# Attention layer of a decoder step on one core: decode queries padded by POOL into the input's place, two turns of cache chunks moved between the last prompt units, one cache copy issued two pairs of heads earlier

## The reference, cut to what matters

```python
DIL_WINDOWS = (128, 512, 2048)
DIL_RATES = (1, 4, 16)

def odd_mixer(x, w_in, w_out, past):
    proj = jnp.einsum('btd,de->bte', x, w_in).reshape(B, T, N_DIL, 3, DIL_HEADS, HEAD_DIM)
    for g in range(N_DIL):
        q, k, v = proj[:, :, g, 0], proj[:, :, g, 1], proj[:, :, g, 2]
        if past is None:
            o, lse = dilated_prompt_attention(q, k, v, win, dil, slopes)
        else:
            k_all = jnp.concatenate([kv_buf[:, :, 0].astype(k.dtype), k], axis=1)
            v_all = jnp.concatenate([kv_buf[:, :, 1].astype(v.dtype), v], axis=1)
            o, lse = strided_window_decode(q[:, :, :, None], k_all, v_all, n_past, win, dil, slopes)
            new.append(jnp.stack([k_all[:, T:], v_all[:, T:]], axis=2))
```

## Time and profile before

| What | us |
|---|---|
| median of three executions | 1773.56 (1771.61 to 1775.28) |
| profiled execution, device time | 1772.61 |
| its span, first to last instruction | 1770.80 |
| prompt part of layer 1 ends (`turn(7)`) | 1003.6 |
| first group's values read by DVE L1951 | 1086.55 |
| second group's values read by DVE L1951 | 1129.36 |

### The profile page before, as it was taken

One profiled execution on the slowest core, in us unless ns is written; L12 is line 12 of the kernel. 1 busy time (PEld: TensorE's weight loads), 2 busy tenths in 40 slices (PEclk: granted clock), 3 DMA queues, 4 the chain that ended last, 5 costly groups with the idle time before them and its releaser, 6 DMA issues.

```text
span 1770.8 us, 29064 instructions
## 1 busy us (share of the span) xinstructions
PE 1639.3 (93%) x11306; PEld 887.4 (50%) x11306; DVE 493.0 (28%) x1318; ACT 440.0 (25%) x847; POOL 260.7 (15%) x663
## 2 busy tenths in 40 slices
PE   7889699999999999989999757879999999999996
PEld 5655444544444454536577544444545454444542
DVE  4342512222221222231022422442222222212224
ACT  1422412222222222231022312242222222222223
POOL 0100321112121211100110200042111121212110
PEclk9958899999999999998999888989999999999998
DMA  9962479999999999949982898428998899999990
GB/s 277 283 231 73 173 287 377 360 354 376 353 371 357 371 359 367 362 153 356 336 340 80 289 327 304 200 112 358 362 372 359 354 376 354 370 359 369 360 368 28
DMA packets 114177, 540.78 MB, mean 305 GB/s; under 512 B 19093, under 2 KB 22933, under 8 KB 79956
## 3 DMA queue, kind: packets, MB, share of 16 engines
q1 hardware_dynamic: 110864, 481.67, 70.7%
q0 software_dynamic: 3200, 58.41, 9.6%
q10 hardware_dynamic: 68, 0.08, 0.0%
HBM read 535.69 MB, written 59.58 MB: 336 GB/s over the span
## 4 chain that ended last, share of the span: by engine, by line
PE 86%; DVE 6%; DMA 4%; ACT 1%; issue 1%; SPq 1%; DVEq 0%; PEldq 0%; ACTq 0%
PE ps L1279 25%; PE ps L1299 13%; PE ps L1254 12%; PE ps L1309 10%; PE ps L1563 6%; PE ps L454 3%; PE ps L1569 2%; PE ps L978 2%; PE ps L1316 2%; DMA arena<-in_router_bias 2%; DMA arena<-in_cache_dil_kv 1%; PE ps L1806 1%; PE ps L1685 1%; PE ps L1888 1%; PE ps L1264 1%
## 5 line engine op out<-in xcount | busy, mean ns | idle before, releaser
L1279 PE MATMUL ps<-ring,arena 128*64 128x512 f32 x2048 | 450.4, 592 | 1.6 <-ACT arena L1366 1.6
L1279 PEld LDWEIGHTS ps<-ring,arena 128*64 128x64 f32 x2048 | 147.8, 137 | 292.2 <-issue 290.4
L1299 PE MATMUL ps<-ring,arena 128*64 128x512 f32 x1024 | 233.8, 598 | 0.9 <-ACT arena L1371 0.9
L1254 PE MATMUL ps<-arena 128*128 128x128 bf16 (+1 forms) x3584 | 223.3, 219 | 2.1 <-issue 2.1
L1254 PEld LDWEIGHTS ps<-arena 128*128 128x128 bf16 (+1 forms) x3584 | 207.2, 98 | 18.7 <-issue 18.0
L1309 PE MATMUL ps<-arena 128*128 128x512 bf16 x768 | 179.8, 384 | 5.6 <-DVE arena L1437 5.6
L1366 ACT ACTIVATE arena<-ps 128x512 f32<-128x512 f32 x128 | 76.4, 597 | 359.4 <-PE ps L1254 359.4
L1242 POOL TENSOR_SCALAR arena<-arena 128x64 bf16<-128x64 f32 x384 | 160.2, 444 | 14.0 <-POOLq L1239 14.0
L1234 POOL COPY arena<-misc 128x64 f32 x64 | 15.3, 238 | 847.3 <-POOLq L1231 847.3
L1309 PEld LDWEIGHTS ps<-arena 128*128 128x128 bf16 x768 | 70.4, 98 | 134.7 <-issue 53.1
L1413 DVE CAST arena<-ps 128x256 bf16<-128x256 f32 x64 | 27.2, 425 | 390.7 <-PE ps L1264 390.7
(11 more groups left out here) (323 smaller groups left out, 1366.8 us busy)
## 6 DMA issues: line engine op xcount, KB each, us to landing
ring<-in_w_exp_gate SPq DMA_DIRECT2D x128, 1024.0 KB, 8.0
ring<-in_w_exp_up SPq DMA_DIRECT2D x128, 1024.0 KB, 10.2
ring<-in_w_exp_down SPq DMA_DIRECT2D x128, 1024.0 KB, 7.1
out_dil_kv_sample<-in_cache_dil_kv POOLq DMA_DIRECT2D x8, 4080.0 KB, 35.3
ring<-in_w_in_odd SPq DMA_DIRECT2D x6, 3072.0 KB, 22.6
out_dil_kv_sample<-in_cache_dil_kv POOLq DMA_DIRECT2D x8, 2032.0 KB, 30.2
ring<-in_cache_dil_kv SPq DMA_DIRECT2D x4, 2048.0 KB, 11.5
ring<-in_cache_dil_kv SPq DMA_DIRECT2D x32, 256.0 KB, 8.7
```

The costliest lines, as they stand in the source:

```text
L1254: ins = pe.matmul(ps[:, TOK_A + hf, (c % 4) * P:(c % 4 + 1) * P], lhs, pm[0:m, q, k // 3, :], start=k == 0, stop=k == 6)
L1279: ins = pe.matmul(ps[64 * u:64 * u + CAP, WORK, :], MO["xg"][:, c, u * CAP:(u + 1) * CAP], w[:, c], start=c == 0, stop=c == NC - 1)
L1299: ins = pe.matmul(ps[64 * u:64 * u + CAP, TOK_A + hf, :], MO["hT"][:, j, 64 * u:64 * u + CAP], w[:, j, hf * BANK:(hf + 1) * BANK], start=j ...
```

## The change

- `qz1` now lies in `xT`, and POOL makes it: `od_dec_prepare(pool)` runs in POOL's program ahead of the stores of pair 3. It waits for the last query tile, clears `xT`, copies the 24 blocks; then it waits for the stores of pair 2 (`s_kst[0]` at 16*12) and copies `kns`, which takes their place.
- The four chunks of the first cache now all lie in `W`, over `kst`, `p_s` and `p_pt`. SP issues them after the last `turn(7)` and the stores of pair 3.
- PE turns chunk 0 between pauses 14 and 15, and chunk 1 in two halves around the last values. Turned tiles go through PSUM banks 2 and 3, scores of the decode part to banks 0 and 1. ACT and DVE copy them between their own pauses; the first such copy waits for `s_qz1` at 26 and for the last unit's scores.
- POOL issues the copy of the middle cache ahead of the stores of pair 2, with no wait of its own.

```diff
-        qz1 = W[:, 0:3072].rearrange("p (g i r) -> p g i r", g=3, i=4)
+        qz1 = xflat.rearrange("p (g i r) -> p g i r", g=3, i=4)
...
-        g1c = [xflat[:, 0:D], xflat[:, D:2 * D], xflat[:, 2 * D:3 * D], W[:, 3584:3584 + D]]
+        g1c = [W[:, 384 + b * D:384 + (b + 1) * D] for b in range(4)]
...
             pause(14)
+            od_dec_turn(pe, 0, 0)
             pause(15)
+            od_dec_turn(pe, 0, 1, (0, 1))
             values(15)
+            od_dec_turn(pe, 0, 1, (2, 3))
             turn(7)
...
+            pool.wait_ge(s_op, LAST_QK + 1)
+            pool.memset(xflat, 0.0).then_inc(s_qz1, 1)
...
+            pool.wait_ge(s_kst[0], 16 * 12)
+            pool.tensor_copy(kns, OD["k"][:, :, :, NPR:NT]).then_inc(s_qz1, 1)
...
+            if g == 0 and ck == 0:
+                eng.wait_ge(s_qz1, 26)
+                eng.wait_ge(s_s, 32)
...
-            sp.wait_ge(s_op, LAST_QK + 1)
+            sp.wait_ge(s_ot, 2 + 8)
+            sp.wait_ge(s_kst[1], 16 * 12)
             for b in range(4):
-                if b == 3:
-                    sp.wait_ge(s_qz1, 26)
                 sp.dma_start(chunk_of(b, 4), rows_of(b, 4)).then_inc(s_g1[b], 16)
...
+                if i == 2:
+                    shift(o[names[2][0]], a[names[2][1]], names[2][2])
+                if i == 3:
+                    od_dec_prepare(pool)
                 for part in range(3):
                     item_copied(pool, at_item["k", i, part])
...
-            pool.wait_ge(s_ring[1][slot_of(9)], loaded(1, 9))
-            shift(o[names[2][0]], a[names[2][1]], names[2][2])
...
-                    od_dec_prepare(v)
                     od_dec_dve(v)
```

More of the change, by code:

```diff
@@ L1488, in build @@
         mx1, nb1, den1, rin1 = (gbf[:, 11 * P + 16 * k:11 * P + 16 * k + 16] for k in range(4))
-        qz1 = W[:, 0:3072].rearrange("p (g i r) -> p g i r", g=3, i=4)
-        kns = W[:, 3072:3456].rearrange("p (g i n) -> p g i n", g=3, i=4)
-        sm1 = W[:, 3456:3472]
+        xflat = xT[:, :, :].rearrange("p c t -> p (c t)")
+        qz1 = xflat.rearrange("p (g i r) -> p g i r", g=3, i=4)
+        kns = W[:, 0:384].rearrange("p (g i n) -> p g i n", g=3, i=4)
+        sm1 = W[:, 4480:4496]
         QK = OD["qk"].rearrange("p a g n -> p (a g n)")
@@ L1498, in build @@
         o_all, o_own, o_twice = W[:, 4608:5120], W[:, 5120:5184], W[:, 5184:5312]
-        xflat = xT[:, :, :].rearrange("p c t -> p (c t)")
-        g1c = [xflat[:, 0:D], xflat[:, D:2 * D], xflat[:, 2 * D:3 * D], W[:, 3584:3584 + D]]
+        g1c = [W[:, 384 + b * D:384 + (b + 1) * D] for b in range(4)]
         s1 = mixT[:, 4:8, :].rearrange("p j t -> p (j t)")[:, 0:DEC_W]
@@ L1599, in od_stage_pe @@
             pause(14)
+            od_dec_turn(pe, 0, 0)
             pause(15)
+            od_dec_turn(pe, 0, 1, (0, 1))
             values(15)
+            od_dec_turn(pe, 0, 1, (2, 3))
             turn(7)
-            items_copied(pe, len(OD_ITEMS) - 1)
+            pe.wait_ge(s_qz1, 26)
             pe.wait_ge(s_otc, 2 + 8)
@@ L1635, in od_items_copy @@
             pause(14)
+            od_dec_keys(eng, copy, parity, 0, 0)
             pause(15)
+            od_dec_keys(eng, copy, parity, 0, 1)
         def od_stage_dve(v):
@@ L1767, in odd_prompt_act, with od_dec_prepare @@
             return exps, copy, turned
[L1769 to L1775, removed]
+        def od_dec_prepare(pool):
+            pool.wait_ge(s_op, LAST_QK + 1)
+            pool.memset(xflat, 0.0).then_inc(s_qz1, 1)
+            pool.wait_ge(s_qz1, 1)
+            for n in (LAST_QK, LAST_QK - 1, LAST_QK - 2):
+                item_copied(pool, n)
             q8 = qz1.rearrange("p g i (b h t) -> p g i h b t", h=NH, t=TS)
@@ L1781, in od_dec_prepare, with od_dec_turn @@
                         rows = slice(HD * s, HD * s + HD)
-                        v.tensor_copy(q8[rows, g, i, 2 * i + s], src[rows]).then_inc(s_qz1, 1)
-            v.tensor_copy(kns, OD["k"][:, :, :, NPR:NT]).then_inc(s_qz1, 1)
-            v.wait_ge(s_qz1, 26)
+                        pool.tensor_copy(q8[rows, g, i, 2 * i + s], src[rows]).then_inc(s_qz1, 1)
+            pool.wait_ge(s_qz1, 25)
+            pool.wait_ge(s_kst[0], 16 * 12)
+            pool.tensor_copy(kns, OD["k"][:, :, :, NPR:NT]).then_inc(s_qz1, 1)
         def kt_copied(n):
             return s_kt_copied[n % 2], n // 2 + 1
[L1789 to L1795, removed]
+        def od_dec_turn(pe, g, ck, bbs=range(4)):
+                for bb in bbs:
                     n = 28 * g + 4 * ck + bb
+                    if n < 2:
+                        items_copied(pe, len(OD_ITEMS) - 1)
                     if g == 0 and ck == 0:
@@ L1805, in turn, with od_dec_pe @@
                     for i in range(4):
-                        ins = pe.transpose(ps[:, n % 2, i * P:(i + 1) * P],
+                        ins = pe.transpose(ps[:, 2 + n % 2, i * P:(i + 1) * P],
                                            chunk_of(4 * g + bb, ck)[:, i * P:(i + 1) * P], ident)
                     ins.then_inc(s_kt, 1)
-            turn(0, 0)
+        def od_dec_pe(pe):
+            turn = lambda g, ck: od_dec_turn(pe, g, ck)
             for g in range(2):
@@ L1816, in scores @@
                         pe.wait_ge(s_sm1, 1)
-                    bank, col, gg = (2, ck * P, 1) if ck < 4 else (3, (ck - 4) * P, 0 if ck == 4 else 2)
+                    bank, col, gg = (0, ck * P, 1) if ck < 4 else (1, (ck - 4) * P, 0 if ck == 4 else 2)
                     for i in range(4):
@@ L1826, in od_dec_pe @@
                 for ck in range(7):
-                    if ck < 6:
+                    if ck < 6 and (g or ck):
                         turn(g, ck + 1)
@@ L1833, in od_dec_pe @@
                     for i in range(4):
-                        ins = pe.matmul(ps[:, 3, 384 + 32 * gg:416 + 32 * gg], qz1[:, gg, i, P * g:P * g + P],
+                        ins = pe.matmul(ps[:, 1, 384 + 32 * gg:416 + 32 * gg], qz1[:, gg, i, P * g:P * g + P],
                                         kns[:, gg, i, :], start=i == 0, stop=i == 3)
@@ L1842, in od_dec_pe @@
                     pe.wait_ge(s_otc, 2 + 8)
-                    od_out_pe(pe, 0, range(3))
+                    od_out_pe(pe, 1, range(3))
                 pe.wait_ge(s_ex1, g + 1)
@@ L1871, in od_dec_pe @@
                     pe.sem_inc(s_free[1][slot_of(6 + 4 * g + bb)], 1)
-            od_out_pe(pe, 1, range(3))
+            od_out_pe(pe, 0, range(3))
             outputs_t(pe, 1)
@@ L1911, in od_dec_keys @@
                     eng.wait_ge(s_sd1, 8 * g + max(ck - 1, 0))
-                copy(kt1[:, ck % 2, bb], ps[:, n % 2, :].rearrange("p (i n) -> p i n", i=4)).then_inc(
+                copy(kt1[:, ck % 2, bb], ps[:, 2 + n % 2, :].rearrange("p (i n) -> p i n", i=4)).then_inc(
                     s_kt_copied[parity], 1)
@@ L1924, in od_dec_dve @@
             for g in range(2):
-                for ck in range(g, 7):
+                for ck in range(1 if g else 2, 7):
                     od_dec_keys(v, v.tensor_copy, 1, g, ck)
@@ L1941, in od_dec_dve @@
                 step(v.scalar_tensor_tensor(out=s1, in0=dd1, scalar=row_slope,
-                                            in1=banks(2, DEC_W), op0=ALU.mult, op1=ALU.add))
+                                            in1=banks(0, DEC_W), op0=ALU.mult, op1=ALU.add))
                 step(v.tensor_reduce(c(0), s1, AX.X, ALU.max))
@@ L2136, in _ @@
                 load(1, 6 + b, parts + [(chunk_of(b, ck), rows_of(b, ck)) for ck in (5, 6)])
-            sp.wait_ge(s_op, LAST_QK + 1)
+            sp.wait_ge(s_ot, 2 + 8)
+            sp.wait_ge(s_kst[1], 16 * 12)
             for b in range(4):
-                if b == 3:
-                    sp.wait_ge(s_qz1, 26)
                 sp.dma_start(chunk_of(b, 4), rows_of(b, 4)).then_inc(s_g1[b], 16)
+            sp.wait_ge(s_qz1, 26)
             sp.dma_start(dd1, a["c_odd"][0]).then_inc(s_dd1, 16)
```

## The result

| | before | changed |
|---|---|---|
| median, us | 1772.59 (4 executions) | 1755.40 (4 executions) |
| ratio of the two, 95% interval | 1 | 0.9904 (0.9888 to 0.9920) |
| profiled execution, device time | 1772.61 | 1752.50 |
| its span | 1770.8 | 1750.7 |

The change makes the kernel 17.2 us faster; the interval of the ratio allows 14.2 to 19.9 us. The forecast was 25.6 us (1747) in a range from 1737 to 1758, so the sign and the range hold and the size is too large by 8 us. Part of the span's 20.1 us comes from ahead of the change: pair 1's last store was issued at 945.12 and is now issued at 943.22, 1.9 us earlier, in a stretch where both programs are the same. Instants of the two profiles differ by that much.

The account below looks back on a forecast made before the run. It took SP's transfers, starved by the middle cache's copy, as the bound. Transfer 9 at 1013, tail 9.7 and first group 38.45 put the values' reader at 1061.2 instead of 1086.55: 25.3 off 1772.6, forecast 1747, range 1737 to 1758.

Parts of the forecast that it names:

- The bound and the mechanism: Layer 1: the copy starves SP's queue; issued at 945.7 it lands near 1002, and PE waits for transfer 9 until 1013.
- One sign of being wrong: PE standing where `s_qz1` decides, over 4 us waiting for chunks or second keys, or slower prompt tiles between 946 and 981.
- The packet count that gave 1013: Transfers 8 and 9: of 1536 packets, 1000 remain at 1002 and need 9.2 us; about 2 us added for engines finishing unevenly.
- POOL's part: `qz1` memset 2.9 us and 24 copies 5.7 us, then `kns`; `s_qz1` at 26 at about 1006, hidden behind 1013.
- Rival 4: Slower than before because POOL's small copies are the bound; 1790 at 3 us each; 3%.
- The prompt's tail: Last weights to last turn: 4.3 us, plus tiles 3.0, DVE copy 0.7, waits 0.5, clock 1.2; 9.7 together, ending at 1022.7.
- The first group: First scores to the values' reader: 22.35, 7.0 and 9.1, sum 38.45 us, so read at 1061.2 instead of 1086.55.
- under cover: After the prompt: SP's chunk 4 covered by 1 us, second group's keys by a hair; range keeps up to 6 us for both.
- The sum: Whole kernel: 25.3 us off 1772.6 gives 1747.3; the shown median is 0.95 above the profiled execution; stated as 1747.
- Rival 1: Queues share by bytes, so stores behind the copy and `kns` decide, `s_qz1` at 1008 to 1013; 1744 to 1748; 10%.

Follow-up runs that it names:

- run 3: The changed kernel with the middle cache's copy one place earlier still, behind the first cache's copies after pair 0: 1733.61 us, ratio 0.9793.
- run 8: The changed kernel once more without any further edit, beside a repeat of the copy's move alone: 1748.13 us, ratio 0.9893.
- run 1: The kernel before with only the middle cache's copy moved ahead of pair 2's stores: 1752.27 us, ratio 0.9902.
- run 2: The changed kernel with the copy back at its old place behind the last stores: 1771.67 us, ratio 1.0007.
- run 7: The changed kernel with chunks 0 and 1 turned after the prompt again: 1745.44 us, ratio 0.9861.
- run 4: The changed kernel with the same copy in pieces of 4064 bytes, 16 DMAs of 1016 KB instead of 8 of 2032 KB: 1751.19 us, ratio 0.9894.

## Why the prediction came out as it did

**The bound and the mechanism: right.** The instants are those of the first profile of the changed kernel. DMA starvation by the copy was what PE waited for, and the copy's move into an empty stretch was the one thing that counted. The copy was forecast to land at 1000 to 1004 and landed at 1003.3; transfer 8 at 1003 to 1006 and landed at 1005.0; transfer 9 at 1013 and landed at 1013.6; pair 2's stores at 1004 and landed by 1006.2; `s_qz1` at 1006 and the new keys were copied at 1006.3. PE slowed down nowhere between 946 and 981. One sign of being wrong did show in part: PE stood 10.5 us for the tile behind `s_qz1`. But `s_qz1` was in 7 us ahead of transfer 9, as forecast, so it did not set the time. The packet count that gave 1013 is the step to learn.

**POOL's part: right, hidden.** Its memset took 2.68 us and the 24 copies 6.27, against 2.9 and 5.7. Rival 4, a POOL that is the bound, is out.

**The prompt's tail: the term that was mis-sized in this execution.** The forecast had 9.7 us from transfer 9 to the last turn, 1.2 of it for the lower clock. It took 12.6 (1013.6 to 1026.2). In run 3 the stretch from the last weights on takes 6.8 us with the clock up and here 11.7, so the clock cost 4.9 there, not 1.2; it stayed down for the whole tail. The other terms were about 1 us too large: 8.5 without the clock, against some 7.4 (6.8 and 0.6 for one tile, an estimate from run 3). In run 8 the same program took 9.0 from transfer 9 to the last turn (1014.38 to 1023.36), and the clock cost 1.3. So 1.2 was right for one execution and 3.7 short for the other, and no row of the kernel before could tell which would come.

**The first group: nearly right.** 39.2 us from the first scores to the reader, against 38.45. SP's chunks and the second group's keys stayed under cover, as forecast: no wait for them shows, and the chunks landed 6.3 us after the last issue at the latest.

**The sum.** On one axis, transfer 9's time is 2.5 us later than forecast (0.6 as the instants stand, 1.9 since this execution ran ahead), the tail 2.9 longer, the group 0.8 longer, and 0.4 lie between the last turn and the first scores, for which the forecast had nothing: together 6.6, which covers the 6.5 us between 25.3 and the profile's 18.8. In run 8 the forecast 1013, 1022.7 and 1061.2 came out as 1014.3, 1023.4 and 1061.8, and the profiled execution took 1748.17 us against the sum's 1747.3. The median gain was 20.5 us there and not the sum's 25.3, since the kernel before ran at 1768.61 beside it, 4.0 us under its profiled execution. No profile of those executions was kept, so where these 4 us lie is open. One slip of the sum is apart from this: 1747.3 and the 0.95 us that the text adds make 1748.2, not 1747.

**What the prediction didn't ask.** It named the new wait correctly, with prompt and SP queued behind it, and took its price as given. It never worked out the same sum without the parts that cause it. Runs 1, 2 and 7 do: the copy's move alone gives 0.9902, the other parts alone 1.0007, the change without the moved turns 0.9861. The moved turns put some 6 to 8 us back. Rival 1's shares by bytes don't occur: 15.55 MB go beside 1.39. The Trainium skill (DMA: Bandwidth & Descriptors, Queues, rings and completion order) has the engine change queues packet by packet, and the counts of 357 to 357 and 495 to 490 agree. It gives a typical packet 9 to 17 descriptors; no view here counts descriptors, so that figure is neither borne out nor refuted. The prediction's step from it to shares by bytes would also need descriptors of one size in both queues.

**The better version.** Run 3 has the lowest ratio shown: 0.9793 of before, 1.0 to 1.1% under the changed kernel. What it does is one place in POOL's order. DMA was idle before from 925 to 945 too, which the change didn't use:

```profile
925.00:945.00 20.00, 19.83 (x99) 15.06 (x97) 5.14 (x11) 3.60 (x9) 3.09 (x5) 1.00 0.05 16
```

Started early enough to use it, the copy ends at 968.1, before the last ring transfer is issued at 982.1.

## What to carry to other kernels

When a long copy moves into an idle stretch, ask which other queue has transfers due before the copy ends, and count packets, not bytes: beside packets of 44 KB the queue with 4 KB packets moved 0.03 MB a us here instead of 0.41. Work that is moved forward takes its waits along, so put it behind what it doesn't need to hold up, or finish its inputs first; and when a change has several parts, work the sum out with each part alone, because the same two parts were worth 11 us in one arrangement and nothing in another, where the moved turns cost about what the padding on POOL saved (experiments 1 and 7). And before a term is called mis-sized, read a second execution of the same program: two profiles of the changed kernel differ by 3.6 us in the one stretch that the clock governs.

## What the runs showed that was not expected

The clock's return to its upper level varied widely, between two executions of one program. In the first profile of the changed kernel it stood at 0.50 from 1004 to 1028, though PE was busy 12.8 of the last 15 us of that:

```profile
1013.00:1018.00 5.00, 4.39 (x21) 4.39 (x22) 0.69 (x1) 0.81 (x1) 0.00 (x0) 0.50 0.02 5
1018.00:1023.00 5.00, 5.00 (x26) 5.00 (x26) 0.69 (x1) 0.87 (x2) 0.00 (x0) 0.50 0.00 0
1023.00:1028.00 5.00, 3.41 (x37) 2.74 (x39) 1.05 (x3) 0.88 (x2) 0.00 (x0) 0.50 0.16 48
1028.00:1032.00 4.00, 3.75 (x56) 2.84 (x52) 1.30 (x2) 1.19 (x2) 0.00 (x0) 0.85 1.00 384
```

In run 8, the same program, PE resumed at 1014.38 after the same 5.0 us of waiting and did the same work, and the clock was up from 1018 on:

```profile
1013.00:1018.00 5.00, 3.62 (x18) 3.62 (x18) 0.69 (x1) 0.81 (x1) 0.00 (x0) 0.50 0.08 28
1018.00:1023.00 5.00, 3.85 (x35) 3.61 (x34) 1.75 (x4) 1.47 (x3) 0.00 (x0) 1.00 0.00 0
```

The kernel before and run 1, below, had it back some 3 to 5 us after PE resumed (at 1038.43 and 1017.86):

```profile
1038.00:1042.00 4.00, 3.57 (x41) 2.74 (x42) 0.69 (x1) 0.00 (x0) 0.00 (x0) 0.54 1.01 345
1042.00:1046.00 4.00, 3.75 (x54) 2.85 (x52) 1.38 (x2) 1.54 (x3) 0.00 (x0) 1.00 0.88 314
```

```profile
1017.00:1022.00 5.00, 4.14 (x18) 3.51 (x19) 1.37 (x4) 1.19 (x2) 0.00 (x0) 0.50 0.66 240
1022.00:1027.00 5.00, 4.55 (x57) 3.21 (x55) 2.16 (x4) 1.79 (x3) 0.00 (x0) 0.97 1.02 314
```

So the instructions of the tail are not the reason: run 8 has the same ones, and in run 4 they run at the upper level from 1020 on, after PE resumed at 1017.24. What made the one execution different stays open.
